# Gate products of a linear-attention scan from short-format parts that are split in the projection stage; a new load order and other q sums in the first stage

## The reference, cut to what matters

```python
p_lat = jnp.split((h_lat @ w_in).astype(jnp.float32), idx, axis=-1)   # q,k,v,z,a,b, q,k,v,gate,lr
# GDN q and k: conv of 3 taps, SiLU, then
q = _l2norm(_heads(q, GDN_HEADS)) * (GDN_DK ** -0.5)
def merge(o_a, z, o_b, gate, dtype):
    y_a = _merge_heads(_rms_norm(o_a, gdn_norm)) * jax.nn.silu(z)
    y_b = _merge_heads(_rms_norm(o_b, gla_norm)) * jax.nn.silu(gate)
    return (jnp.concatenate([y_a, y_b], axis=-1).astype(w_out.dtype) @ w_out).astype(dtype)
```

## Time and profile before

| | us |
|---|---|
| median of 3 runs (1650.60 to 1655.95) | 1654.94 |
| the profiled execution, its own time | 1656.5 |
| its span | 1654.8 |
| PE busy | 1602.6 (97%) |
| DVE busy | 1230.4 (74%) |

### The profile page before, as it was taken

How to read it: one execution, slowest core, us unless ns; L and a number is a source line. 1 busy time by engine, 2 the same in 40 slices (tenths; PEclk the granted TensorE clock), 3 DMA queues, 4 the chain that set the end, 5 groups by cost and what they waited for, 6 DMA issues and landing times.

```text
span 1654.8 us, 20720 instructions
## 1 busy us (share of the span) xinstructions
PE 1602.6 (97%) x8142; PEld 1195.8 (72%) x8142; DVE 1230.4 (74%) x1760; ACT 561.5 (34%) x892; POOL 453.3 (27%) x436
## 2 busy tenths in 40 slices
PE   7999999999999989999999999999999999999997
PEld 1545555995599955656588888888888887887886
DVE  4587888599766678888876599889888898434435
ACT  1544333543243322222745322222222223233332
POOL 5011101121234246665234433323333333000000
PEclk9999999999999999999999999999999999999999
DMA  9266554864398640000523211111111112522332
GB/s 353 69 234 221 166 191 149 250 163 113 94 289 236 184 153 26 13 26 14 204 96 116 69 51 52 51 45 45 52 51 51 47 44 89 191 89 90 114 129 88
DMA packets 201373, 194.79 MB, mean 118 GB/s; under 512 B 40101, under 2 KB 155119, under 8 KB 201148
## 3 DMA queue, kind: packets, MB, share of 16 engines
q1 hardware_dynamic: 194592, 190.00, 36.0%
q10 hardware_dynamic: 6396, 3.20, 0.7%
q0 software_dynamic: 288, 0.27, 0.1%
HBM read 151.32 MB, written 42.12 MB: 117 GB/s over the span
## 4 chain that ended last, share of the span: by engine, by line
PE 56%; DVE 5%; issue 1%; ACT 1%; POOL 1%; DMA 0%; ACTq 0%; POOLq 0%; DVEq 0%
PE PS L2139 10%; PE PS L2135 10%; PE PS L2137 10%; PE PS L2174 5%; PE PS L2176 5%; PE PS L2178 5%; PE PS L1993 4%; PE PS L2008 2%; DVE Qbd L2436 2%; PE PS L2095 1%; PE PS L2097 1%; PE PS L2096 1%; PE PS L2030 1%; DVE AT L2452 1%; DVE Ex L2417 1%
## 5 line engine op out<-in xcount | busy, mean ns | idle before, releaser
L2607 DVE SCALAR_TENSOR_TENSOR acc<-PS,fcol,acc 128x945 f32<-128x945 f32 (+2 forms) x176 | 215.2, 1222 | 29.1 <-ACT acc L2266 23.5
L2607 DVE SCALAR_TENSOR_TENSOR act<-PS,fcol,act 128x945 f32<-128x945 f32 (+2 forms) x176 | 215.2, 1223 | 21.6 <-ACT act L2266 16.2
L2135 PE MATMUL PS<-h2hi,whi 128*128 128x512 f32 x704 | 219.5, 389 | 0.0
L2139 PE MATMUL PS<-h2hi,wlo 128*128 128x512 f32 x704 | 219.3, 389 | 0.0
L2137 PE MATMUL PS<-h2lo,whi 128*128 128x512 f32 x704 | 219.3, 389 | 0.0
L418 PE MATMUL PS<-hT,wq 128*128 128x512 f32 (+1 forms) x432 | 163.1, 537 | 0.0
L1945 POOL TENSOR_TENSOR wlo<-wu,whi 128x1024 fp32r<-128x1024 f32 x44 | 106.4, 2421 | 206.9 <-ACT whi L2259 206.6
L2139 PEld LDWEIGHTS PS<-h2hi,wlo 128*128 128x128 f32 x704 | 132.1, 188 | 27.4
L2135 PEld LDWEIGHTS PS<-h2hi,whi 128*128 128x128 f32 x704 | 132.1, 188 | 27.4
L2137 PEld LDWEIGHTS PS<-h2lo,whi 128*128 128x128 f32 x704 | 132.1, 188 | 27.4
L2618 DVE TENSOR_TENSOR wrlo<-wr,wrhi 128x1024 fp32r<-128x1024 f32 x41 | 50.2, 1225 | 129.6 <-ACT wrhi L2356 129.6
(11 more groups left out here) (312 smaller groups left out, 2856.8 us busy)
## 6 DMA issues: line engine op xcount, KB each, us to landing
wm<-in_w_mod_dram SPq DMA_DIRECT2D x24, 1024.0 KB, 7.5
wu<-in_w_up_dram SPq DMA_DIRECT2D x44, 512.0 KB, 3.7
wr<-in_w_down_dram SPq DMA_DIRECT2D x44, 512.0 KB, 3.4
wq<-in_w_in_dram SPq DMA_DIRECT2D x12, 512.0 KB, 9.4
gdn_x_image<-ztile SPq DMA_DIRECT2D x10, 516.0 KB, 9.9
gdn_xt_image<-ztile SPq DMA_DIRECT2D x10, 516.0 KB, 8.1
GR<-gdn_gc_rows SPq DMA_DIRECT2D x20, 256.0 KB, 5.3
gdn_w_image<-Wm SPq DMA_DIRECT2D x20, 256.0 KB, 4.4
```

The costliest lines, as they stand in the source:

```text
L2135: pe.matmul(PS[:, b + half, :], whi[k][u][:, kk, :], h2hi[:, 4 * half:4 * half + 4, kk, :], start=(kk == 0), stop=False)
L2139: mm = pe.matmul(PS[:, b + half, :], wlo[k][u][:, kk, :], h2hi[:, 4 * half:4 * half + 4, kk, :], start=False, stop=(kk == KT - 1))
L2607: tp = v.scalar_tensor_tensor(out=t_[:, r0:r1, c0:c1], in0=up[:, r0 + dr:r1 + dr, c0 + dc:c1 + dc], scalar=tap_col(j, k, f), in1=t_[:, r0: ...
```

## The change

Five things are done together.

1. **Gate weights split in the first block.** SP loads the 8 column blocks raw (`wst`), POOL rounds them to `wsthi` (fp32r) and subtracts (`wstlo`); SP stores both parts to DRAM (8 MB). SP's loop also waits for the store of each low part before it loads the raw block three further on.
2. **h split in the first block.** ACT rounds each of the 8 slices of hT (`h_high`), POOL subtracts (`h_low`) and issues the stores of both parts (8 MB). The old spill of hT on SP is gone.
3. **Gate products from the parts.** Each float32 product becomes three fp32r products. The units are ordered with all 8 blocks for token half 0 first and then all for half 1, so that hL holds one half in two parts; each block's weights (two parts, 1 MB) are loaded twice.
4. **First loads** in the order v = 1, 0, 2, x tiles 0 and 1, v = 3, x tiles 2 and 3, x tiles 4 to 7, wq(q), wq(k), context, wq(v).
5. **q sums of the first head** by one plain float32 product with ones, straight from the squares.

The places of the tiles in memory, the order of the slices of `wo` (WORD) and two buffers for the first GDN rows (`ogf`) follow from it.

```diff
-                for v in range(3):
+                for v in (1, 0, 2):
                     for kh in range(2):
                         modulation(v, kh)
-                x_rows(0)
+                x_rows(0, 0, 2)
                 modulation(3, 0)
                 modulation(3, 1)
...
+                sp.wait_ge(s_xt, 3)
+                for j in range(3):
+                    gate_raw(j)
+                for j in range(2 * H):
+                    sp.wait_ge(s_gwh, j + 1)
+                    sp.dma_start(gwhi_dram[j], wsthi[j % 2][:, :, :].bitcast(F32)).then_inc(s_gwhs[j % 2], 16)
+                    sp.wait_ge(s_gwl, j + 1)
+                    sp.dma_start(gwlo_dram[j], wstlo[j % 3][:, :, :].bitcast(F32)).then_inc(s_gwls, 16)
+                    if j + 3 < 2 * H:
+                        sp.wait_ge(s_gwls, 16 * (j + 1))
+                        gate_raw(j + 3)
                 sp.wait_ge(s_xt, NT)
                 sp.wait_ge(s_qd, 1)
                 rest(0)
...
+                for j in range(2 * H):
+                    g.wait_ge(s_gwi[j % 3], 16 * (j // 3) + 16)
+                    if j >= 2:
+                        g.wait_ge(s_gwhs[j % 2], 16 * (j // 2))
+                    g.tensor_copy(wsthi[j % 2][:, :, :], wst[j % 3][:, :, :]).then_inc(s_gwh, 1)
+                    g.wait_ge(s_gwh, j + 1)
+                    g.tensor_tensor(wstlo[j % 3][:, :, :], wst[j % 3][:, :, :], wsthi[j % 2][:, :, :], ALU.subtract).then_inc(s_gwl, 1)
...
+                def h_low(k):
+                    u = HSET[k]
+                    g.wait_ge(s_hsh, k + 1)
+                    g.tensor_tensor(hstlo[u][:, :], hT[:, k, 0:LAT], hsthi[u][:, :], ALU.subtract).then_inc(s_hsl, 1)
+                    g.dma_start(hhi_dram[:, k, :], hsthi[u][:, :].bitcast(F32)).then_inc(s_hs[u], 16)
+                    g.wait_ge(s_hsl, k + 1)
+                    g.dma_start(hlo_dram[:, k, :], hstlo[u][:, :].bitcast(F32)).then_inc(s_hs[u], 16)
+                LOWS = {(0, 0): (0, 1), (0, 1): (2, 3), (1, 0): (4, 5, 6, 7)}
...
                 def sums(kind, h):
+                    if h == 0 and kind == 0:
+                        pe.wait_ge(s_csq[0], 1)
+                        for b, (t0, n) in enumerate(PARTS[0]):
+                            mm = pe.matmul(PS[:, BANK[0] + b, 0:n], ones[:, :], csq[:, t0:t0 + n], start=True, stop=True)
+                        mm.then_inc(s_css[0], 1)
+                        return
...
+                def h_high(k):
+                    u = HSET[k]
+                    if k == 0:
+                        a.wait_ge(s_hta, 2 + NL)
+                        a.wait_ge(s_htv, 2 + NL)
+                        a.wait_ge(s_xt, NL)
+                    elif k <= 2:
+                        a.wait_ge(s_gwls, 32 * H)
+                        a.wait_ge(s_gwhs[0], 16 * H)
+                    else:
+                        a.wait_ge(s_hs[u], 32 * HSET[0:k].count(u))
+                    a.activation(hsthi[u][:, :], hT[:, k, 0:LAT], ACT.Copy).then_inc(s_hsh, 1)
...
                     evac(0, h)
+                    if h == 0:
+                        h_high(1)
                     silu(0, h)
                     evac(1, h)
                     root(0, h)
+                    if h == 0:
+                        h_high(2)
+                        h_high(3)
                     silu(1, h)
...
                 def conv(kind, h):
                     n = CO if kind else LAT
                     v.wait_ge(s_raw[kind], h + 1)
+                    if kind and h == 0:
+                        v.wait_ge(s_hs[2], 32)
...
+                    if u == 8:
+                        for i in range(3):
+                            if i < 2:
+                                sp.wait_ge(s_gu, i + 1)
+                            else:
+                                sp.wait_ge(s_m4, 8)
+                            h_again(1, i)
...
                     for k in range(k0, k1):
-                        mm = pe.matmul(PS[:, 3, :], ws4[n % 2][:, k, :], hL[half][:, k, :],
-                                       start=(k == 0), stop=(k == KT - 1))
+                        if blk_ == 0 and k in (0, 2, 4):
+                            pe.wait_ge(s_hr[r][k // 2], 32)
+                        pe.matmul(PS[:, 3, :], zwhi[u % 2][:, k, :], hLhi[:, k, :], start=(k == 0), stop=False)
+                        pe.matmul(PS[:, 3, :], zwhi[u % 2][:, k, :], hLlo[:, k, :], start=False, stop=False)
+                        mm = pe.matmul(PS[:, 3, :], zwlo[u % 2][:, k, :], hLhi[:, k, :], start=False, stop=(k == KT - 1))
```

217 lines of the change are left out of this document (140 added, 77 removed).

## The result

| | kernel before | changed kernel |
|---|---|---|
| median of 6 runs (range) | 1655.5 us (1650.6 to 1660.3) | 1668.8 us (1663.7 to 1671.6) |
| ratio, with its 95% interval | 1 | 1.0079 (1.0060 to 1.0098) |
| the profiled execution, and its span | 1656.5, 1654.8 | 1667.0, 1665.2 |
| first product of head 0 | 46.92 | 43.74 |
| v's products of head 0 start | 89.08 | 106.23 |

The forecast was 1654.6 in 1644 to 1663. The table is a balance. The first block loses 18.2 us (it ended at 281.88, not at about 270 as the text ahead says), the GLA block gives back 4.3, and the way from it to the feed-forward stage loses 1.9 more: 15.8 us. The medians show 13.4 and the two profiled spans 10.4, since in this pair the stretches that no kernel here changes came out 5.4 us shorter.

The account below looks back on a forecast made before the run. PE was taken as the bound after the start's data wait, with DVE near it in the GLA block. Gains of 9.3 us there and losses of 9.0 in the first block gave -0.3: 1654.6 us, range 1644 to 1663.

Parts of the forecast that it names:

- the two cancel: Likeliest case: the GLA block's gain of 9.3 us and the first block's loss of 9.0 cancel, 1654.6 us; chance 0.43.
- rival 3: First block's split: SP's wait on each low store adds up round trips, 7.7 us a round, 1661 us; chance 0.26.
- T: First block: time when all 16 gate parts are in DRAM, for which ACT's copy of h's slice 1 waits; 90.1 us.
- part C: First block: gate-weight split and what waits for it; v's products 7.3 us later, plus 1.7 us for PE's clock.
- part A: GLA block: gate products as three short-format products, 9.3 us gained, between 5 and 13.
- B, the start: First block: new load order moves the first product from 46.92 to about 44.1, 2.8 us, lost again in the wait.
- rival 2: First block: split done in time with 5.2 us rounds, part C costs 0.5 to 1 us, 1646.5 us; chance 0.31.
- The clock: First block: PE's clock falls after its wait for q's squares, 1.7 us lost, with 2.65 as the bound above.
- Downstream of C I add nothing: First block after the split: DVE's wm and k convolution are 8 to 9 us late, as PE is; no further cost.
- Middle bodies: GLA block's six middle bodies: shorter DVE waits gain 0.86 us per body, 5.2 us in all.
- First body: GLA block's first body, PE's until ACT's exp: 2.8 us gained from cheaper gate products.
- The stall: GLA block: PE waits 1.5 us for the last 2 MB chunk of h's second half, mostly hidden, 0.5 us lost.

Follow-up runs that it names:

- lag: Changed kernel with SP waiting for the low store of the round before, not the one just issued: 1661.0 us, ratio 1.0031.
- filler: Changed kernel with 20 float32 products into an unused PSUM bank before PE's wait for q's squares: 1670.4 us, ratio 1.0091.
- fine_h: Changed kernel with the second half of h loaded in four chunks of 1 MB: 1663.6 us, ratio 1.0058.
- late_copy: Changed kernel with ACT's copy of slice 1 of h moved behind the root of q in head 0: 1667.5 us, ratio 1.0076.
- late_all: Changed kernel with head 0's work that waits for the split moved behind what PE needs, two wm loads earlier: 1667.9 us, ratio 1.0080.
- pool_holds: all_mended with DRAM image fills moved to heads 2 and 3, and POOL's sixth gate block held until DVE ends head 0's q convolution: 1654.9 us, ratio 0.9989.
- late_all_lag: late_all with SP's wait for the low store one round late, as in lag: 1659.9 us, ratio 1.0033.
- all_mended: late_all_lag with the second half of h in four chunks, as in fine_h: 1654.9 us, ratio 0.9995.
- mended_2: all_mended with image fills in heads 2 and 3, head 1's q evacuation earlier, second wm piece later, two more wo slices first: 1649.0 us, ratio 0.9952.
- one_part: Changed kernel with fine_h's chunks, two more wo slices first, only one of eight gate blocks and h slices split: 1644.3 us, ratio 0.9925.

## Why the prediction was wrong

The likeliest case, "the two cancel", failed and rival 3, the slower one, came true. Its mechanism was stated right, with too low a chance and too small a price. The step that failed is T, the end of the split in part C: 98.0 us for 90.1. The second is the size of part A, 4.3 us gained for 9.3. By the steps:

- **B, the start: right.** 43.74 for 44.1 forecast, the last row at 27.41 for 27.5.
- **C, T = 90.1: the step that failed.** It was 98.0. The first low part was stored at 56.8, where the forecast had 53.7: POOL could begin 2.5 us later, and its first two operations took 4.06 us for 3.5. The four rounds took 29.1 for 25.2 us. Of these 3.9 us, three rounds of 6.6 to 6.8 for 6.3 give 1.3, and the one round of 8.9 gives 2.6; its cause is open. The last block took 12.2 for 11.2. lag shows that the rounds were long by SP's wait and not by bandwidth. The rule of the Trainium skill that the prediction set beside its own price ("DMA: Bandwidth & Descriptors", the anatomy of one DMA; 5.6 us a round) would have been further off. The page gives its fit for transfers that GpSimd issues, and these are SP's. That T mattered so much is the other half. The sum was steep in it, one for one from 82.8 on, and a forecast with so steep a slope at its likeliest value should have given the slower case more than 0.26. Two of its bounds don't follow from its terms either: with a round of 5.2 us T is 85.7 (85.0 with the rounding at 0.96), so v's products start near 92, and rival 2 would lose 2 to 3 us in C, not 0.5 to 1; T = 83.3 is reached by neither.
- **The clock: 2.7 us and not 1.7.** I took the price of a sparse stretch; filler gives 1.8 for the sums and 0.9 for v's products. By the Trainium skill ("TensorE: Matmul & The Clock Gate", "What's actually happening") an idle array falls to half its clock and starts again at half. The prediction priced this rule at 2.65 us and did not take it; the 2.7 us of this trace agree with it.
- **"Downstream of C I add nothing": right for this profile, and partly by luck.** There is no second wait in the block here, since everything is late together. But fine_h, with the same lists in the first block, waits 5.05 us in head 1. late_copy, late_all and pool_holds show how close the next ones stand: 13.2, 8.8 and 8.0 us. That also strikes rival 2, which put the whole gain at T under 86. In late_all_lag v's products start at 89.35, as before the change, and head 1 waits 6.5 us.
- **A, the GLA block: 4.3 us and not 9.3.** A product's price was right: three start in 0.70 us (from 719.70 on), for 0.68.
  - Middle bodies: the gain is 1.1 us each, 6.6 in all for 5.2 forecast (156.18 for six in place of 158.51, with the stall of 4.27 taken out); DVE's wait of 0.86 shrank by 0.66 and not by 0.25.
  - First body: 0.4 for 2.8. Its first 16.4 us run at a granted clock of 0.65 (0.79 before), and PE's gate products begin 17.7 us after the block's start in place of 16.3. Most of this is the clock, which differs from one execution to the next: in late_copy, late_all and all_mended, where this stretch runs at 0.79 as before, the body with the same lists takes 38.6 to 38.7 us in place of 40.95, a gain of 2.3. In lag, late_all_lag, mended_2 and one_part it takes 40.3 to 40.5. Why the clock differs there stays open. At its end DVE is the bound already, PE waits 0.53 us for it.
  - Last body: 1.5 for 1.8.
  - The stall: 4.3 for 0.5. The load of 2 MB landed 8.7 us after its first issue (717.55) for 7 forecast, PE waited 3.46 us for 1.5, and "mostly hidden, because DVE is one level behind" is what failed. DVE has no slack once PE's waits are gone, and a late PE is late for all.
- **Not priced at all: the weights of the output projection.** They lie in the place of h, whose last reader is now later. The way from the GLA block to the feed-forward stage takes 109.74 us for 107.82. PE is idle for 1.35 us of it (0.29 before), in small waits behind ACT's rounding of `wo` and DVE's rest of `y`; the other 0.9 us are longer records. mended_2, which loads two more slices of `wo` first, takes 107.80 there and waits 2.33 us for the modulation sums just before: the wait has moved and is not removed. That the weights' place is the cause is so far argued from this one run.

Together: C and B +18.2 for +9.0, A -4.3 for -9.3, the weights +1.9 for 0. That is 16.1 us more than forecast in these stretches; the medians came out 14.2 above the forecast.

## What to carry to other kernels

Work that is "off the critical path" on idle engines has a deadline wherever an engine's in-order list or a shared place in memory ties it to the path. Count all strands that hang on its end, since taking one away only shows the next. A loop that stores and reloads should wait for the store of the round before, not for the one just issued (4.75 against 7.27 us a round here). Before such work is placed, sum up the bytes of every transfer in that stretch; here moving 4 MB of zero fills out of the way was worth 7 us.

## What the runs showed of the hardware

- POOL's large float32 work and DVE's beside it slow one another: two `SCALAR_TENSOR_TENSOR` of 128x1024 take 5.2 to 5.4 us in place of 2.6, a `TENSOR_SCALAR` 2.44 in place of 0.75, and POOL's subtraction 3.2 to 3.5 in place of 2.35. The Trainium skill has this in "GPSIMD Engine Reference", "Specifications": POOL shares its SBUF interfaces with DVE and contends with DVE instructions in a two-port mode or with two SBUF inputs. The trace agrees for these instructions, and adds the size.
- The length of one wait does not tell whether PE's clock falls: 3.71 us at 84 in the kernel before left the sums and v's products at full speed, 3.06 us at 81 in late_copy made the four q records 3.78 us long in place of 1.98, with 1.2 us more on v's, 12.3 us in lag cost 1.7 us in all, and 20.1 us in the changed kernel cost 2.7.
- One round of the split took 8.9 us with the DMA engines at 0.09 of their time from 76 to 80; POOL waited 5.5 us for a high store of 0.5 MB that was issued at 70.7. What held that store stays open.
